# Gate tiles taken beside attention, ranking rounds between low parts, band bias ahead, and a split copy-out in a decoder layer kernel

## The reference

```
ys = stack([y_a, y_d, y_f, y_s])
proj = einsum('blnc,ncd->blnd', ys, w_branch)            # 4 x (1024 x 256) @ (256 x 1024)
gates = sigmoid(g)                                       # g = h @ w_in[:, gate columns]
mix = sum(gates * proj, axis=2) @ w_o
# dsa: score = sum_h w_h * relu(q_h . k); the 256 largest scores of a row keep their keys
# dsa and swa logits carry a bias that is linear in the distance (swa: outside the band -1e30)
# fox: logits + F_q - F_k, causal; softmax in all three
```

## Time and profile before

| | before |
|---|---|
| median of 3 runs | 1734.74 us |
| the profiled execution | 1735.29 us, of which span 1733.5 us |
| PE busy | 1680.1 us, 97% of the span |
| PEld busy | 1397.3 us, 81% |
| DVE busy | 1055.2 us, 61% |
| POOL busy | 822.4 us, 47% |
| ACT busy | 613.3 us, 35% |
| mean granted TensorE clock | 0.992 |

### The profile page before, as it was taken

One profiled execution on the slowest core, in us unless ns is written; L12 is line 12 of the kernel. 1 busy time (PEld: TensorE's weight loads), 2 busy tenths in 40 slices (PEclk: granted clock), 3 DMA queues, 4 the chain that ended last, 5 costly groups with the idle time before them and its releaser, 6 DMA issues.

```text
span 1733.5 us, 22877 instructions
## 1 busy us (share of the span) xinstructions
PE 1680.1 (97%) x8072; PEld 1397.3 (81%) x8072; DVE 1055.2 (61%) x1756; ACT 613.3 (35%) x1104; POOL 822.4 (47%) x537
## 2 busy tenths in 40 slices
PE   5999999999999999989999999999999999999997
PEld 4877878787888888879888888888888888888886
DVE  7745745556999999947486445843553454345337
ACT  5544336374222222246423455332223223222323
POOL 2421130102436565620288434675567656655755
PEclk9999999999999999999999999999999999999999
DMA  8131141010111111340575403120112012111205
GB/s 342 37 85 47 51 115 35 16 52 17 61 46 46 45 46 45 112 103 1 217 273 171 170 14 133 37 73 30 66 49 68 29 48 73 48 48 48 73 25 207
DMA packets 37455, 138.87 MB, mean 80 GB/s; under 512 B 4624, under 2 KB 4624, under 8 KB 37392
## 3 DMA queue, kind: packets, MB, share of 16 engines
q1 hardware_dynamic: 35152, 130.70, 21.7%
q0 software_dynamic: 2240, 7.34, 1.9%
HBM read 118.10 MB, written 13.63 MB: 76 GB/s over the span
## 4 chain that ended last, share of the span: by engine, by line
PE 68%; issue 11%; POOL 10%; DVE 4%; DMA 4%; ACT 2%; SPq 1%; POOLq 0%; ACTq 0%; DVEq 0%
PE ps L639 19%; PE ps L640 18%; PE ps L641 18%; POOL w_t L1713 5%; PE ps L863 4%; PE ps L842 2%; PE ps L766 1%; DMA raw<-in_w_ffn 1%; PE ps L767 1%; POOL w_f L1728 1%; DMA region_a<-in_x 1%; PE ps L670 1%; POOL raw L1731 1%; POOL slot_c L1713 1%; DVE region_c L1904 1%
## 5 line engine op out<-in xcount | busy, mean ns | idle before, releaser
L639 PE MATMUL ps<-h_t,w_t 128*128 128x512 f32 x1112 | 437.7, 394 | 3.3 <-DVE h_t L1896 1.6
L641 PE MATMUL ps<-h_t,w_t 128*128 128x512 f32 x1112 | 433.6, 390 | 0.0
L640 PE MATMUL ps<-h_t,w_t 128*128 128x512 f32 x1112 | 433.5, 390 | 0.0
L639 PEld LDWEIGHTS ps<-h_t,w_t 128*128 128x128 f32 x1112 | 209.4, 188 | 49.7 <-issue 5.5
L641 PEld LDWEIGHTS ps<-h_t,w_t 128*128 128x128 f32 x1112 | 209.1, 188 | 44.0
L640 PEld LDWEIGHTS ps<-h_t,w_t 128*128 128x128 f32 x1112 | 209.4, 188 | 42.8 <-issue 0.7
L1564 POOL TENSOR_TENSOR w_t<-raw,w_t 128x1280 fp32r<-128x1280 f32 (+1 forms) x50 | 145.9, 2918 | 198.2 <-ACT w_t L1154 197.9
L2265 DVE TENSOR_TENSOR y_f<-ps,y_f 128x512 f32<-128x512 f32 x120 | 80.7, 686 | 217.5 <-PE ps L641 217.5
L1713 POOL TENSOR_TENSOR w_t<-raw,w_t 128x512 fp32r<-128x512 f32 x80 | 110.2, 1383 | 136.7 <-ACT w_t L1452 136.7
L1950 DVE MAX8 top<-region_b 128x8 f32<-128x384 f32 (+5 forms) x192 | 157.9, 882 | 17.6 <-issue 17.0
L1953 DVE MATCH_REPLACE8 region_b<-top,region_b 128x384 f32<-128x384 f32 (+5 forms) x192 | 166.1, 876 | 0.0
(11 more groups left out here) (286 smaller groups left out, 3345.4 us busy)
## 6 DMA issues: line engine op xcount, KB each, us to landing
raw<-in_w_ffn SPq DMA_DIRECT2D x46, 512.0 KB, 3.9
raw<-in_w_gates SPq DMA_DIRECT2D x32, 640.0 KB, 3.9
region_b<-in_w_ada SPq DMA_DIRECT2D x33, 512.0 KB, 4.5
region_d<-in_w_ffn SPq DMA_DIRECT2D x20, 512.0 KB, 4.0
raw<-in_w_z SPq DMA_DIRECT2D x18, 512.0 KB, 3.4
region_a<-in_x SPq DMA_DIRECT2D x8, 512.0 KB, 14.9
h_f<-in_w_ada SPq DMA_DIRECT2D x8, 512.0 KB, 8.1
raw<-in_w_o SPq DMA_DIRECT2D x8, 512.0 KB, 3.6
```

What stands on the lines that cost most here:

```text
L639: pe.matmul(o, a_hi, m_hi, start=first, stop=False, skip_group_check=more)
L640: pe.matmul(o, a_hi, m_lo, start=False, stop=False, skip_group_check=more)
L641: return pe.matmul(o, a_lo, m_hi, start=False, stop=last, skip_group_check=more)
```

## The change

Seven things move.

1. **Gate tiles beside swa attention.** The generator that deals out gate matmuls between the last units takes a number of half tiles. At the end of the second stretch three halves (12 parts, dealt 1, 2, 2, 2, 3, 2 with nothing behind the last `turn_out`) take the place of two (8 parts). The third half goes to bank 6; the second half of that tile follows in bank 7 (`gate_second`). For it ACT's `split_hi` of the second tile moves into its attention loop, five units in, and POOL's `split_lo` ahead of the low part of A's output. At the end of dsa attention the parts stay as they are.
2. **S's last gate tile behind the dsa queries.** The eighth gate tile of S becomes T_LAST and is computed after the two query tiles, right before dsa attention. The queries' stacks move to the other half of `y_t`, and D's output takes the place of S's. Only `z[1..6]` have to be in DRAM before keys and units use their places; `z[7]` has a semaphore of its own, for which ACT waits before unit 1's copy.
3. **One low buffer for both query tiles**, so DVE waits for the first tile's moves before it makes the second's low part.
4. **The distance table** goes to `region_c` (free once S's output is split), not to `region_d`, and is loaded earlier.
5. **The band bias of swa** is loaded when four fewer fox units have had their logits, in two pieces, the first head's into a place of its own.
6. **Rounds of block 5** (768 columns) between the convolution's products, behind `forget_spread`, and between the low parts of the fox tiles: 2 + 2 + (2 + 2 + 2 + 2 + 1) = 13 of its 32 rounds. The rounds that are left after swa attention run on six, then five, then four blocks at once. The dsa low parts are now made ahead of the masks.
7. **The copy-out of a swa unit is split**: ACT copies heads 0 and 1 (bank 0), DVE heads 2 and 3 (bank 1), in a new step `turned_heads` between `biased(u + 1)` and `group_norm(u - 2)`.

```diff
+SIDE_BLOCK = 5
+SIDE_ROUNDS = {(0, 1): 2, (1, 0): 2, (2, 0): 2, (2, 1): 2, (3, 0): 1}
+FILL = {3: (1, 2, 2, 2, 3, 2), 2: (1, 1, 1, 1, 0, 1), 0: (0,) * 6}
@@ SP
-            sp.wait_ge(s_logit, U_SWA)
-            sp.dma_start(region_d[:, :], window_bias).then_inc(s_table, 16)
+            sp.wait_ge(s_logit, U_SWA - 4)
+            sp.dma_start(spare[:, 2 * P:4 * P], window_bias[:, 0:2 * P]).then_inc(s_table, 16)
+            sp.dma_start(region_d[:, 2 * P:L], window_bias[:, 2 * P:L]).then_inc(s_table, 16)
...
+            sp.wait_ge(s_ys, 1)
+            sp.dma_start(far, distance).then_inc(s_table, 16)
+            tile_load(T_LAST, w_gates[3 * KT - 1])
+            for dt in range(1, KT - 1):
+                spill(dt, s_spill)
+            tile_load(T_GD, w_gates[3 * KT])
+            spill(KT - 1, s_spill_last)
+            tile_load(T_GD + 1, w_gates[3 * KT + 1])
@@ PE
                 if kind == "swa":
+                    pe.wait_ge(s_pt_dve, u - U_SWA + 1)
...
                     turn(u)
                     if u >= end - 2:
-                        next(beside)
+                        fill(parts_at[2 * (u - end + 2)])
                     if u - 2 >= u0:
                         turn_out(u - 2)
                     if u > u0:
                         values(u - 1)
                     if u >= end - 2:
-                        next(beside)
+                        fill(parts_at[2 * (u - end + 2) + 1])
+                fill(parts_at[4])
                 turn_out(end - 2)
                 values(end - 1)
-                next(beside)
+                fill(parts_at[5])
                 turn_out(end - 1)
-                for _ in beside:
-                    pass
+                fill(4 * KT)
...
+            def gate_second(T, buf):
+                for _ in gate_half(7, T, 1):
+                    pass
+                for half in range(2):
+                    pe.wait_ge(s_zf, 2 * T + half - 1)
+                    tile_half(ps[:, 2 + half, :], T % 2, half, KT, BT, y_hi(buf), y_lo(buf)).then_inc(s_z, 1)
...
             gate_first(T_AFS, 0)
-            gate_tile(T_AFS + 1, 0)
+            gate_second(T_AFS + 1, 0)
...
-            gate_pairs(T_AFS + 2 * KT, 0)
-            z_group(T_DSA, T_GD - T_DSA)
+            gate_pairs(T_AFS + 2 * KT, 0, KT // 2 - 1)
+            gate_tile(T_DSA - 1, 0)
+            z_group(T_DSA, 2)
+            gate_tile(T_LAST, 0)
@@ ACT, attention
+                    if gate is not None and u == u0 + 4:
+                        split_hi(gate + 1, n=GT)
+                    if u == U_DSA + 1:
+                        act.wait_ge(s_spill_last, 16)
-                        dst, src = window_cols(pt[u % 2], b), window_cols(bank, b)
+                        dst, src = (window_cols(a, b)[:, 0:2] for a in (pt[u % 2], bank))
@@ POOL
-            gate_pairs(T_AFS + 2 * KT, False)
+            gate_pairs(T_AFS + 2 * KT, False, KT // 2 - 1)
+            split_lo(T_DSA)
+            gate_tile(T_DSA - 1, KT - 2, False)
+            split_lo(T_DSA + 1)
+            stack_moves(T_DSA)
+            split_lo(T_LAST)
...
+            stack_moves(T_DSA + 1)
+            split_lo(T_GD)
+            gate_tile(T_LAST, KT - 1, False)
@@ DVE
+            def turned_heads(u):
+                b = units[u][1]
+                dve.wait_ge(s_t, u + 1)
+                dve.wait_ge(s_pv, u - 1)
+                dst, src = (window_cols(a, b)[:, 2:4]
+                            for a in (pt[u % 2], ps[:, 0:2, :].rearrange("p a n -> p (a n)")))
+                dve.tensor_copy(dst, src).then_inc(s_pt_dve, 1)
...
                         biased(u + 1)
+                    if units[u][0] == "swa":
+                        turned_heads(u)
                     if u >= u0 + 2:
                         group_norm(u - 2)
...
+                for half in range(2):
+                    stack_lo_half(T, half)
+                    if T == T_FOX + 1 and half:
+                        forget_sums(0)
+                    elif (T - T_FOX, half) in SIDE_ROUNDS:
+                        top_k([SIDE_BLOCK], SIDE_ROUNDS[T - T_FOX, half])
```

More of the change, by code:

```diff
@@ L55 @@
 T_IDX, T_CONV, T_FOX, T_SWA, T_AFS = 0, 3, 9, 13, 16
-T_DSA = T_AFS + 3 * KT
-T_GD = T_DSA + 2
+T_DSA = T_AFS + 3 * KT - 1
+T_LAST = T_DSA + 2
+T_GD = T_LAST + 1
 T_WO = T_GD + KT
@@ L460, in window_cols, with window_bias_cols @@
             return v[:, :, P:2 * P] if b == 0 else v
+        def window_bias_cols(hh, b):
+            at = spare[:, 2 * P:4 * P] if hh == 0 else region_d[:, 2 * hh * P:2 * (hh + 1) * P]
+            return at[:, P:2 * P] if b == 0 else at
         def logits_ps(u):
@@ L493, in gate_tiles @@
         def gate_tiles(T):
-            return T_AFS <= T < T_DSA or T_GD <= T < T_WO
+            return T_AFS <= T < T_DSA or T_LAST <= T < T_WO
         def width(T):
@@ L876, in turn_out, with attention, fill @@
                 mm.then_inc(s_turned, 1)
-            def attention(u0, n, gate=None):
+            def attention(u0, n, gate=None, halves=0):
                 end = u0 + n
-                beside = gate_beside(gate)
+                beside, parts_at = gates_beside(gate, halves), FILL[halves]
+                def fill(parts):
+                    for _ in range(parts):
+                        next(beside, None)
                 logits(u0)
@@ L995, in column_sums @@
                     mm.then_inc(s_mod, 1)
-            gate_tile(T_WO - 1, 1, read=s_h_read, between=column_sums)
+            gate_tile(T_WO - 1, 0, read=s_h_read, between=column_sums)
             for k in range(KT):
@@ L1294, in exponentials, with attention @@
                                    accum_out=den[:, g % 4, col:col + 1]).then_inc(s_exp, 1)
-            def attention(u0, n):
+            def attention(u0, n, gate=None):
                 end = u0 + n
@@ L1646, in _ @@
             pool.tensor_tensor(y_lo(0), ya_back[:, :, :], y_hi(0).bitcast(F32), ALU.subtract).then_inc(s_ya, 1)
-            gate_pairs(T_AFS, True)
+            gate_tile(T_AFS, 0, True)
+            split_lo(T_AFS + 2, n=GT)
+            gate_tile(T_AFS + 1, 1, True)
+            with order.loop(KT // 2 - 1, 0) as i:
+                for j in range(2):
+                    split_lo(T_AFS + 2 + j + 1, i, 2, GT)
+                    gate_tile(T_AFS + 2 + j, 2 + j, True, i)
             pool.wait_ge(s_ys_hi, 1)
@@ L2122, in _ @@
             attention(U_FOX + 2 * TT, 2 * TT + TT)
-            top_k(range(KB0, TT), rounds - rounds_done[KB0])
-            top_k(range(KB0 + 1, TT), rounds - rounds_done[TT - 1])
-            assert all(n == rounds for n in rounds_done.values())
+            while any(n < rounds for n in rounds_done.values()):
+                left = [b for b in rounds_done if rounds_done[b] < rounds]
+                top_k(left, min(rounds - rounds_done[b] for b in left))
+            for T in range(T_DSA, T_LAST):
+                stack_lo(T)
             for b in range(KB0, TT):
                 order.mark(dve.tensor_scalar(sc_at[b], sc_at[b], TAKEN / 2, -BIG, ALU.is_gt, ALU.mult))
-            for T in range(T_DSA, T_GD):
-                stack_lo(T)
             order.wait()
-            dve.wait_ge(s_table, 32)
-            dve.wait_ge(s_spill, 16 * (KT - 1))
+            dve.wait_ge(s_table, 48)
+            dve.wait_ge(s_spill, 16 * (KT - 2))
             attention(U_DSA, HEADS * TT)
```

120 lines of the change are left out of this document (65 added, 55 removed).

## The result

| | before | after |
|---|---|---|
| median | 1734.61 us (18 runs, 1731.14 to 1739.37) | 1739.03 us (18 runs, 1735.02 to 1743.41) |
| profiled execution, span | 1733.5 us | 1739.8 us |

The ratio is 1.0025, with a 95% interval from 1.0016 to 1.0034. The forecast was 1723.1, some 11.6 us faster; the kernel came out 4.4 us slower, outside the range.

A forecast was written before the change was run, and what follows sets the result against it. TensorE, 97% busy, was taken as the bound. Gains 2.4 + 6.3 + 4.0 less 0.5 and 0.6 made 11.6 us, from 1735.3 to 1723.7, median 1723.1; range 1716.5 to 1731 (the forecast case's own 1719.5 to 1727, chance 0.50).

The forecast's parts named there:

- Split copy-out: Swa units: DVE's half copy fits, no cost in the middle, 1 us at unit 38, counted inside the bias term's 2.4.
- swa bound by DVE: Swa units: DVE's chain is longer than summed, 0.7 us more in each of 7 units, 1728 us; chance 0.16.
- The clock: PE around the waits: a wait costs twice, idle time and half-speed matmuls behind it, at most some 5.4, 7 and 9 us.
- Bias ahead: Start of swa: the bias loaded four fox units earlier nearly removes PE's wait; gain 2.4 us, bounds 0.5 to 3.5.
- Three halves: End of swa: a third half of gate matmuls covers PE's waits there; gain 6.3 us, bounds 4 to 7.2.
- Third gate tile: Gates after swa: the third tile is needed 8.2 us after `gate_first` instead of 13.7; loss 0.5 us, 0 to 1.5.
- S's last tile: Start of dsa: the gate tile covers the move, DMA and keys; gain 4.0 us, bounds 1 to 5.5.
- Side rounds: Block 5's rounds before and between fox tiles: loss 0.6 us, bounds 0 to 3.5; without them PE would wait later.
- The slower rival: Between fox low parts: rounds take 3.5 us or more, not 2.4, and PE waits; 1738 to 1742 us, chance 0.06.
- Collision at the start of dsa: Unit 1's bias: DVE stands behind POOL, unit 1 slips 1.5 to 3 us, half speed behind it; 1726.5 us, chance 0.13.

The follow-up runs named there:

- norm_first: The changed kernel with DVE's norm of unit u - 2 and store of u - 3 ahead of the split copy-out of unit u: 1721.48 us.
- lo_ahead: The changed kernel with DVE's store of u - 3 ahead of the copy-out, norm still behind, and PE's values(u - 1) ahead of turn_out(u - 2): 1720.92 us.
- bias_late: norm_first with the load of the window bias waiting for the first windowed logits, as in the kernel before: 1727.82 us.
- two_halves: act_whole with two halves of gates beside the last windowed units, in place of three, and the third's ACT and POOL steps as before: 1727.91 us.
- act_whole: The changed kernel without the split copy-out; ACT copies all four heads, as before: 1720.42 us.
- no_last: The kernel before with three gate halves, the bias ahead and the side rounds; no split copy-out, S's last tile ahead of the queries: 1726.99 us.
- no_side: norm_first without the 13 rounds of block 5 in the first half of the kernel: 1729.68 us.
- split_only: The kernel before with the split copy-out alone, in the place and order of the changed kernel: 1749.14 us.
- turn_out_late: The changed kernel with PE's values(u - 1) ahead of turn_out(u - 2), DVE's order unchanged: 1742.25 us.

## Why the prediction was wrong, step by step

**Split copy-out: the step that failed.** The prediction named what is queued behind `turned_heads`, the norm, the store and the bias, and then followed only one chain through it, from the transposes of u to those of u + 2: 7.9 us against 8.1 of TensorE's work. That chain did fit; norm_first and lo_ahead have the same operations and 4.05 to 4.1 us a unit. The binding chain was the short one: transposes of u, copy-out 0.69, norm 0.84, and `turn_out(u - 2)`, the very next instruction on TensorE, with nothing between to cover it. It has no slack at all, and its idle time could be read off the order written in the kernel: 0.68 and the norm, 1.5 us a unit in the middle. "No cost in the middle and 1 us at unit 38" was in fact 17.1 us in the stage, 7.0 of it idle time and 10.1 half speed. The sum gave this part no bounds of its own either, so the range had no room for it.

**Rival "swa bound by DVE".** It pointed at the right place, DVE's copy uncovered in each unit, and was mis-sized. It took 0.7 a unit (the copy alone, 4.9 in all); it was copy and norm, and half speed behind them. Its name is wrong too: DVE stood idle for 2.24 us in the unit shown.

**The clock.** The prediction knew that a wait costs twice and used it only for waits that go. It didn't ask what waits of 1.5 us, shorter than the 2.04 and 3.47 that were there before, do when they come in every unit: a clock of 0.82 and 0.70 over 40 us, and 10.1 us, more than the idle time itself.

**Bias ahead: right, size low.** 3.5 us (norm_first against bias_late), against 2.4 forecast and bounds of 0.5 to 3.5. The reason for the low value was a share kept back for the split. In after the wait of 2.04 at `turn_out` is 0.40, and the stretch has full clock.

**Three halves: right.** Forecast 6.3, measured 6.3 (two_halves against act_whole, with the steps for the third tile in it). **Third gate tile:** forecast -0.5; gates of no_last are 4.99 us shorter than before's with 5.5 moved out, so 0.5 as well; with the last tile moved too it is 0.1 (gates +5.40 in two_halves, where 5.5 came back).

**S's last tile: right, a little low.** Forecast 4.0, measured 4.6 to 5.0 (no_last against act_whole; before against two_halves). In after unit 1 of dsa was turned 7.64 us after the first logits (771.49, 779.13); 8.1 was forecast, 12.3 it was the earlier trace rows.

**Side rounds: right, and needed.** Forecast -0.6; in the profiles norm_first and no_side reach the first windowed logits at 368.51 and 368.48, so they cost nothing that can be seen. "Without the rounds PE would wait" holds: 6.4 us of wait, and 8.6 in the stage, with matmuls at half speed behind the wait. The rounds ended 14 us ahead of the low part, forecast was 16. The slower rival, rounds at 3.5 us, did not happen: after's rows there have MAX8 at 0.95 to 0.96, as the earlier trace rows, and a round every 2.4 us.

**Collision at the start of dsa: met, without price.** It came twice in after. First at unit 0, where POOL had begun earlier:

```profile
766.05 1.70 POOL L1683 TENSOR_TENSOR region_d<-region_d 128x512 f32<-128x512 f32 x1 [1.01 <-ACT region_d L1381]
766.64 2.20 DVE L2093 SCALAR_TENSOR_TENSOR region_a<-region_c,region_b 128x1024 f32<-128x1024 f32 x1
```

DVE's addition took 2.20 us in place of 1.22, by the rival's own mechanism, but it ended 2.7 us ahead of the first logits (771.49). Then at unit 1:

```profile
773.93 1.28 DVE L2093 SCALAR_TENSOR_TENSOR region_a<-region_c,region_b 128x1024 f32<-128x1024 f32 x1
...
774.21 2.14 POOL L1684 TENSOR_TENSOR region_a<-region_a,region_d 128x512 f32<-128x512 f32 x1
```

DVE took 1.28 us, near the 1.22 of the earlier trace rows, and POOL, which came second, took 2.14 where the median of its 48 instructions of that line is 1.29. By the Trainium skill, page SBUF — State Buffer, section Who interferes with whom, the ports that the two share are an exclusive lock, and the order of issue decides who blocks; the trace agrees (at unit 1 POOL ended 1.1 us after DVE did, and at unit 0 DVE 1.1 us after POOL). At unit 1, where TensorE was near, the loser was the one that it didn't wait for.

**Sum.** Without the split the terms measured are 3.5 + 6.3 + 4.7 = 14.5 us, with the third tile in the 6.3; act_whole gained 14.1 in the two stages and 14.0 by the medians. With the split's 17.1 the stages of after give 2.95 us slower, the medians 4.4; the early part's scatter (2.6 us between the two profiles) is enough for the rest, but that it is the rest is not shown. The forecast's 11.6 was within 3 us of this sum. One term put at zero cost 17.

What stays open: the rest after dsa attention's start is 949 us in before and after and 947 to 948 in the other eleven kernels, among them one built on before (split_only). I take it for scatter, which wasn't tried.

## What to carry to other kernels

An instruction that waits is not priced by its own time but by what stands behind it on its engine and is asked for before the wait ends. Write down for each such item who asks for it and how much work that engine has left in between; where the answer is "its next instruction", the whole of copy and successor is bare, however idle the engine is on average. Then count what half speed adds behind such waits when they come in every unit: here it was 10.1 us beside 7.0 of idle time. Put the waiting instruction last of those that are ready, and look at every consumer: moving only one of them (turn_out_late) moved the wait and gave nothing.

## What the runs showed of the hardware that I had not expected

With waits of 1.5 us in units of 4.4 to 5.8 us, TensorE's granted clock went from 1.00 to 0.82 and 0.70 over 14 and 26 us (levels 1.2 and 2.4 GHz), while with 16 transposes of a constant in each wait it was 1.00 and the kernel was 5 us faster with more work in it. As the clock falls the unit grows, from 5.8 to 7.5 and 9.5 us, although DVE's and ACT's own instructions take as long as before (ACT's half copy 0.60 us in each of these units). Of the 17.1 us that the waits cost in the stage, 7.0 were idle time and 10.1 half speed.
